# A hybrid decoder layer on one core: the gate map stored by groups of four blocks, the residual loaded earlier, the softmax exponential moved up, and the sample tokens' expert rows spread over more groups

## The chip, the cores and the metric

The kernel runs on one core of a Trainium2 chip. The metric is the device time of one execution in microseconds. Three runs of the kernel before gave 5026.5, 5029.96 and 5038.7 us, so the median is 5029.96 us. One further execution was taken with the profiler; its times are those of the trace.

## What is computed

One decoder layer is applied to 512 prompt tokens and 64 sample tokens (576 together, model width 2048): a pooling and retention mixer, a cross-attention over memory tokens, and the PEER expert mixer, with a normalization ahead of each and one at the end. The change lies in the last of them:

```python
def one(xb):
    q = (xb @ peer_wq).reshape(PEER_BLOCK, PEER_HEADS, 2, PEER_HALF)
    s = jnp.einsum('thcd,hckd->thck', q, subkeys)      # 8 heads, 2 x 128 keys
    sv, si = lax.top_k(s, PEER_TOPK)                   # 16 of each
    cand = sv[:, :, 0, :, None] + sv[:, :, 1, None, :]
    ...
    top_s, sel = lax.top_k(cand, PEER_TOPK)            # 16 experts per head
    expert = jnp.take_along_axis(cidx, sel, axis=-1)   # of 16384
    g = jax.nn.softmax(top_s, axis=-1)
    u = jnp.take(peer_u, expert, axis=0)
    act = jax.nn.gelu(jnp.einsum('thkd,td->thk', u, xb), approximate=False)
    vv = jnp.take(peer_v, expert, axis=0)
    return jnp.einsum('thk,thkd->td', g * act, vv)
```

So every token has 128 chosen experts, each with a gate; the result is added to the residual, and the final normalization follows.

## The kernel before

The 16384 experts are 128 blocks of 128. The tokens are handled in two ways. For 320 of them ("dense", `ND`) all experts are computed: the activations of a block by matmul with `uT`, an elementwise product with a map of the gates (zero where an expert was not chosen), and a matmul with `vE`, whose 16 output pieces DVE adds to the residual `X`. For the other 256 (`NG`, two chunks of 128) the activations of all experts are computed, but of `vE` only the chosen rows are used: POOL gathers, for each of the 128 places in a token's list, one row of 2048 values per token (1 MB per gather, `row`, L463), and DVE adds it, times its weight, to `ACC` in PSUM (`add_row`, L1637). The weights come from 256 small gathers (`value`, L453). Weights of all matmuls are split into a high and a low part so that the product keeps float32 accuracy: ACT copies the high part (L882), POOL subtracts to get the low part (`low_part`, L417), and each 128x128 block is multiplied three times (L535, L850).

The stages of this part, one after the other:

1. **Heads**: a loop over eight heads. PE projects the queries, then computes the activations for the 256 tokens, in eight pairs of blocks per head (`tokens_first`, L779; on ACT `gelu_tokens`). DVE finds the top 16. After the loop ACT takes the exponential of the softmax (L1211), DVE normalizes it, PE turns the lists (L811), ACT copies them out, and DVE signals `lists_ready`.
2. **Map**: ten steps (`NPG`) of 32 dense tokens. DVE builds one-hot matrices, PE multiplies them to the gate map (L825), ACT copies it to `STG` (two halves `par`) and stores each half to `pmap` in DRAM (L1231, 2 MB each); in between PE computes the activations of two expert blocks per step, so that ten pairs are done ahead (`LAG`). POOL issues ten values per step.
3. **Groups**: 27 (`QT`) groups of four blocks (`quad`). PE does four projections (two calls of `up`, 192 matmuls), then `down` (192 matmuls, 16 pieces d = 0 to 15). POOL has 16 low parts per group, in the order k = 0 to 15: k = 0 to 7 for the next projections, 8 to 15 for the next `down`; after which k it issues rows and values is written out by hand. Two consecutive k feed one half of a matmul stage, and the four slots of `WS` are used in turn, so that POOL can work on a slot only when PE has left it and ACT has written its high part. ACT and POOL have one queue each, in order; a wait holds all that is behind it.
4. **Tail**: five (`NQ - QT`) groups with `down` alone, since their projections were done ahead; then the final normalization.

The rows: each of the two chunks has 128; each group takes `KR` = 10, so that chunk 0 is spread over groups 0 to 12, chunk 1 over groups 13 to 25, and group 26 and the tail have none. When a chunk is complete, ACT copies `ACC` (`rows_evac`), PE turns it in 16 transposes after d = 13 of that group's `down` (L859), and DVE adds it to `X` (L1699). Five buffers hold rows that are on their way (`NB`).

At the turn from map to groups ACT waits for the last stores to `pmap`, issues the loads for group 0 (`load_quad`, L1241 and L1243), then the four loads of the residual (`load_x` of `x3T`, L293), and then goes on to the first projection's output (`gelu_out`, L1192, whose result `store_gelu` writes to `gel`).

## Time and profile before

| | |
|---|---|
| median of three runs | 5029.96 us (5026.5 to 5038.7) |
| the profiled execution, its own time | 5085.41 us |
| its span | 5083.6 us |
| mean granted TensorE clock | 0.948 of full |
| PE busy / weight load busy | 93% / 89% of the span |
| POOL / DVE / ACT busy | 61% / 45% / 31% |
| moved by DMA | 1033 MB, 203 GB/s on average |
| heads end, map begins | about 2947 to 2957 us |
| map ends, groups begin | about 3250 us |
| first `down` | 3308.06 us |
| groups end, tail begins | about 4907 us |

The profiled execution is 55 us (1.1%) longer than the median. A time in this text is a moment or a duration in its trace; 0 is the start of the span. A busy share is an average over the stages and says little about what ends a stage: that is read from the idle time in front of an instruction and from what ended it.

### The profile page before, as it was taken

The numbers are of one execution on the slowest core, as the hardware profiler recorded it, in microseconds if no ns is written. First come the engines' busy times: TensorE is split into PE (matmuls) and PEld (weight loads), VectorE is DVE, ScalarE is ACT, GpSimd is POOL, SyncE is SP. The second block draws the span as 40 slices with busy tenths as digits, with TensorE's granted clock in tenths as the row PEclk, the third lists the DMA queues.
The fourth block names the chain that finished last, engine by engine and source line by source line (L and its number), as shares of the span: only waits on it lengthen the run. The fifth ranks groups of instructions, "written<-read, shape, count | busy, mean of one in ns | idle before, by whom it ended". The sixth has DMA issues, their size and how long they took to land.

```text
span 5083.6 us, 83212 instructions
## 1 busy us (share of the span) xinstructions
PE 4704.6 (93%) x32243; PEld 4538.4 (89%) x32243; DVE 2306.8 (45%) x3103; ACT 1579.4 (31%) x2182; POOL 3100.8 (61%) x1782
## 2 busy tenths in 40 slices
PE   7978999899899998999999988799999999999997
PEld 7778889889788797999999988699999999999997
DVE  3622222422200115444444445366666666666656
ACT  4411112212211223444444444333333333333333
POOL 6723222224211144777777766589999889998864
PEclk9989889899988899999999988899999999999998
DMA  6533222433343424555555545699999899999954
GB/s 217 181 68 95 85 69 85 131 106 105 122 140 139 153 84 149 176 172 171 174 172 173 174 141 165 217 340 345 347 344 343 323 342 342 341 341 356 362 192 148
DMA packets 466619, 1033.07 MB, mean 203 GB/s; under 512 B 136945, under 2 KB 227185, under 8 KB 433649
## 3 DMA queue, kind: packets, MB, share of 16 engines
q1 hardware_dynamic: 216080, 590.67, 34.9%
q0 software_dynamic: 45056, 268.60, 13.8%
q10 hardware_dynamic: 205280, 170.84, 10.4%
q8 instruction: 159, 2.61, 0.2%
q14 instruction: 44, 0.35, 0.0%
HBM read 935.25 MB, written 94.73 MB: 203 GB/s over the span
## 4 chain that ended last, share of the span: by engine, by line
issue 41%; POOL 33%; PE 17%; DMA 3%; DVE 2%; another core or an unknown queue 1%; ACT 1%; ACTq 0%; POOLq 0%; DVEq 0%; SPq 0%
POOL WS L417 22%; PE PS L850 9%; POOL WS L441 7%; PE PS L535 5%; POOL ROWS L463 2%; DMA AR<-in_vE 2%; PE PS L779 2%; POOL AR L453 2%; PE PS L825 1%; ACT WS L882 1%; DMA RAW<-in_vE 1%; DMA gel<-AR 0%; POOL AR L463 0%; DVE AR L1331 0%
## 5 line engine op out<-in xcount | busy, mean ns | idle before, releaser
L535 PE MATMUL PS<-HL,WS 128*128 128x288 f32 (+2 forms) x16896 | 2409.1, 304 | 121.5 <-issue 41.5
L535 PEld LDWEIGHTS PS<-HL,WS 128*128 128x128 f32 x16896 | 2361.7, 191 | 145.6 <-issue 107.1
L417 POOL TENSOR_TENSOR WS<-RAW,WS 128x1024 fp32r<-128x1024 f32 x490 | 1203.0, 2468 | 1572.9 <-ACT WS L882 1569.9
L850 PE MATMUL PS<-WW,WS 128*128 128x320 f32 x6144 | 944.4, 316 | 77.6 <-POOL WS L417 61.6
L850 PEld LDWEIGHTS PS<-WW,WS 128*128 128x128 f32 x6144 | 925.2, 192 | 96.2 <-issue 81.2
L882 ACT ACTIVATE WS<-RAW 128x1024 fp32r<-128x1024 f32 (+1 forms) x714 | 627.1, 919 | 915.3 <-PE PS L535 279.3
L779 PE MATMUL PS<-WS,HL 128*128 128x256 f32 x6144 | 740.5, 283 | 0.0
L779 PEld LDWEIGHTS PS<-WS,HL 128*128 128x128 f32 x6144 | 738.3, 192 | 0.0
L1637 DVE SCALAR_TENSOR_TENSOR PS<-ROWS,AR,PS 128x2048 f32<-128x2048 f32 x206 | 483.8, 2348 | 73.0 <-DMA ROWS<-in_vE,AR 72.2
L417 POOL TENSOR_TENSOR WS<-AR,WS 128x1024 fp32r<-128x1024 f32 x182 | 450.1, 2478 | 34.2 <-ACT WS L882 33.3
L417 POOL TENSOR_TENSOR WS<-CS,WS 128x1024 fp32r<-128x1024 f32 x144 | 347.5, 2413 | 195.1 <-ACT WS L882 193.4
L1652 DVE TENSOR_TENSOR AR<-AR,PS 128x320 f32<-128x320 f32 x512 | 248.6, 486 | 436.0 <-PE PS L850 433.4
L882 ACT ACTIVATE AR<-PS 128x512 f32<-128x512 f32 (+12 forms) x243 | 169.6, 737 | 842.5 <-PE PS L535 410.5
L882 ACT ACTIVATE WS<-CS 128x1024 fp32r<-128x1024 f32 (+1 forms) x256 | 222.9, 871 | 498.2 <-PE PS L850 255.6
L441 POOL TENSOR_TENSOR WS<-RAW,WS 128x512 fp32r<-128x512 f32 x224 | 302.5, 1379 | 16.1 <-ACT WS L882 15.3
L453 POOL DMA_INDIRECT AR<-gelg,AR x256 | 249.4, 974 | 70.6 <-issue 65.4
L882 ACT ACTIVATE WS<-AR 128x1024 fp32r<-128x1024 f32 (+1 forms) x294 | 259.7, 888 | 93.1 <-DMA AR<-in_vE 35.8
L1541 DVE MAX8 AR<-AR 128x8 f32<-128x128 f32 (+1 forms) x120 | 30.1, 324 | 488.7 <-ACT AR L882 487.5
L463 POOL DMA_INDIRECT ROWS<-in_vE,AR x206 | 200.2, 972 | 31.9 <-issue 24.4
L1192 ACT ACTIVATE AR<-PS 128x320 f32<-128x320 f32 x128 | 56.7, 443 | 459.7 <-PE PS L535 396.2
L1625 DVE TENSOR_TENSOR AR<-AR 128x320 f32<-128x320 f32 x128 | 193.9, 1566 | 0.1
L1637 DVE SCALAR_TENSOR_TENSOR PS<-AR,PS 128x2048 f32<-128x2048 f32 x50 | 117.6, 2353 | 120.7 <-DMA AR<-in_vE,AR 120.7
(160 smaller groups left out, 3196.9 us busy)
## 6 DMA issues: line engine op xcount, KB each, us to landing
RAW<-in_uT SPq DMA_DIRECT2D x256, 512.0 KB
RAW<-in_w_lin SPq DMA_DIRECT2D x218, 512.0 KB
CS<-in_uT SPq DMA_DIRECT2D x128, 512.0 KB
AR<-in_uT SPq DMA_DIRECT2D x128, 512.0 KB
RAW<-in_vE SPq DMA_DIRECT2D x128, 512.0 KB
CS<-in_vE SPq DMA_DIRECT2D x64, 512.0 KB
AR<-in_vE SPq DMA_DIRECT2D x64, 512.0 KB
AR<-in_w_lin SPq DMA_DIRECT2D x46, 512.0 KB
```

Of the source, the lines that this page charges most:

```text
L417: pool.tensor_tensor(WS[:, k, 1, :], raw(k, many, late), WS[:, k, 0, :].bitcast(F32), ALU.subtract)\
L441: pool.tensor_tensor(WS[:, k, 1, half], raw(k, True, True)[:, half], WS[:, k, 0, half].bitcast(F32), ALU.subtract).then_inc(S["split_done" ...
L453: pool.indirect_dma_start(out=GA[:, c, k:k + 1], out_offset=None, in_=values, in_offset=at(EL[:, c, k:k + 1]))\
L463: pool.indirect_dma_start(out=ROWS[b], out_offset=None, in_=rows, in_offset=at(VI[:, c, r:r + 1]))\
L535: ins = mm(to, WS[:, slot + hf, wp, k * P:(k + 1) * P], x, start=first and (wp, xp) == (0, 0), stop=last and wp == 1, skip_group_check=True)
L779: ins = mm(to, HLG[:, c, xp, kb, :], WS[:, 2 * hf:2 * hf + 2, wp, k * P:(k + 1) * P], start=(kb, c, wp, xp) == (0, 0, 0, 0), stop=kb == KB ...
L850: ins = mm(bank(2 + d % 2, ND), WS[:, 2 * (q % 2) + b, vp, 512 * e + P * d4:512 * e + P * (d4 + 1)], W[:, 2 * b + e, wp, :], start=(b, e, ...
L882: copy = lambda out, in_, **kw: act.activation(out, in_, ACT.Identity, **kw)
L1192: act.activation(GO[:, e, :], bank(e, ND), ACT.Gelu).then_inc(S["lin_evac"], 1)
L1625: tt(gi, gi, PP[:, e // 2, :, e % 2, :], ALU.mult).then_inc(S["w_done"], 1)
L1637: stt(ACC, ROWS[b], GA[:, c, r:r + 1], ACC, ALU.mult, ALU.add).then_inc(S["row_done"], 1)
L1652: tt(X[:, d, 0:ND], X[:, d, 0:ND], bank(2 + d % 2, ND), ALU.add).then_inc(S["v_free"], 1)
```

## The change

Four things are changed:

- The map is stored for groups of four blocks: `pmap` is (32, 128, 10, 128) in place of (64, 128, 10, 64), so each piece that a store writes is 128 values instead of 64 (10 stores of 2 MB as before). `STG` now lies in `ROWS4`, where the gathered rows will be; the one-hot matrices and lists move as well.
- That frees the place of `X`: the residual is loaded at the start of the map stage, after `lists_ready`, and not at its end. At the turn to the groups, ACT takes the first two outputs of group 0 before it waits for the stores and issues the loads for group 0. The first row of `vE` can be gathered only when the last store is done, so POOL waits for it after k = 9 of group 0.
- The exponential is issued on ACT ahead of the last pair of blocks of the last head; that head is written outside the loop for it.
- Rows: two in group 0, nine in each of the groups 1 to 26 (chunk 0 up to group 14, chunk 1 from group 15), and 20 in the first four tail groups, five each. DVE adds the tail's after d = 4, 5, 10, 12 and 14. Chunk 1 is turned in the last `down` after d = 5 and added after d = 7, and the squares of the final normalization wait for that (`back_added`).

```diff
-KR = 2 * NB
-QR = -(-P // KR)
+KR = 9
+QA = 15
+FIRST_ROWS = P - KR * (QA - 1)
...
-        pmap = dram("pmap", (NP2, P, NPG, 2 * PG))
+        pmap = dram("pmap", (NQ, P, NPG, 4 * PG))
...
-        AA, BB, STG = ar(1152, 2, 4, P), ar(2176, 2, 4, P), ar(3200, 2, NK, PG)
+        AA, BB = ar(10432, 2, 4, P), ar(11456, 2, 4, P)
+        STG = ROWS4.rearrange("p (s i t) -> p s i t", s=2, i=NK)
...
+            def rows_after(i, k, many):
+
+                for j, (c, r) in enumerate(ROWS_OF[i]):
+                    if k == (10 + 2 * j if i == 0 else many * j // KR if i < QT else many * j // KT_ROWS):
+                        row(c, r)
+
             for i in range(QT):
-                c, first = i // QR, i % QR * KR
                 for k in range(16):
                     low_part(H_UV + 16 * i + k // 4 * 4, k % 4, late=True)
-                    for j in range(KR):
-                        if c < 2 and first + j < P and 8 * j // 5 == k:
-                            row(c, first + j)
+                    if i == 0 and k == 9:
+                        for par in range(2):
+                            pool.wait_ge(S[f"out_p{par}"], 16 + 16 * (NPG // 2))
+                    rows_after(i, k, 16)
...
-                        if back and d == 13:
+                        if back and d == (13, 5)[back - 1]:
                             pe.wait_ge(S["rows_evac"], back)
...
                 for j in range(UPP):
+                    if last and j == UPP - 1:
+                        act.wait_ge(S["soft_in"], 1)
+                        act.activation(CAND.rearrange("p t n -> p (t n)")[:, 0:640], EQ.rearrange("p a n -> p (a n)")[:, 0:640],
+                                       ACT.Exp).then_inc(S["soft_exp"], 1)
                     gelu_tokens(h, j)
...
             copy(IOTA4, IOTA.unsqueeze(1).to_broadcast([P, 4, P])).then_inc(S["gt_evac"], 1)
+            act.wait_ge(S["lists_ready"], 1)
+            load_x(act, x3T)
...
                         if (a, e) == (1, 0) and not first:
                             load_next(i + 1)
+                        if (a, e) == (0, 1) and first:
+                            for par in range(2):
+                                act.wait_ge(S[f"out_p{par}"], 16 + 16 * (NPG // 2))
+                            load_quad(0)
...
-            for par in range(2):
-                act.wait_ge(S[f"out_p{par}"], 16 + 16 * (NPG // 2))
-            load_quad(0)
-            load_x(act, x3T)
...
+                    if q == 0 and i == NQ - 1:
+                        evac_rows(1)
+
+
+            act.wait_ge(S["back_added"], 1)
...
                     if d % 3 == 2:
-                        add_rows(i, (NB + d // 3,))
+                        add_rows(i, (5 + d // 3 if i else d // 3 - 3,))
...
+                    if d in (4, 5, 10, 12, 14):
+                        add_rows(i, ((4, 5, 10, 12, 14).index(d),))
+                    if i == NQ - 1 and d == 7:
+                        add_back(1).then_inc(S["back_added"], 1)
```

**ACT, turn from map to groups.** Before (`gel` stores, `pmap` and `gel` loads, `x3T` loads, then the outputs of group 0; "waits" are semaphores):

```order
L1241 DMA AR<-pmap 128x2x640 [waits out_p1,out_g0,out_p0,out_g1,out_gg1,out_gg0]
L1243 DMA AR<-gel 128x4x320
L293 DMA AR<-x3T 128x4x576 x4
L1192 ACTIVATE AR<-PS 128x320 [waits out_g0,used]
L882 ACTIVATE WS<-RAW 128x1024 [waits raw0]
L882 ACTIVATE WS<-RAW 128x1024 [waits raw1]
L1197 DMA gel<-AR 128x320 [waits lin_evac]
L1192 ACTIVATE AR<-PS 128x320 [waits out_g1,used]
L882 ACTIVATE WS<-CS 128x1024 [waits raw2]
```

And now:

```order
L1206 ACTIVATE AR<-PS 128x320 [waits out_g0,used]
L896 ACTIVATE WS<-RAW 128x1024 [waits raw0]
L896 ACTIVATE WS<-RAW 128x1024 [waits raw1]
L1211 DMA gel<-AR 128x320 [waits lin_evac]
L1206 ACTIVATE AR<-PS 128x320 [waits out_g1,used]
L896 ACTIVATE WS<-CS 128x1024 [waits raw2]
L896 ACTIVATE WS<-AR 128x1024 [waits raw3]
L1211 DMA gel<-AR 128x320 [waits lin_evac]
L1260 DMA AR<-pmap 128x1280 [waits out_g0,out_g1,out_p1,out_p0]
L1262 DMA AR<-gel 128x4x320
```

The wait for the stores stands behind the first two outputs, and the four loads of `x3T` are gone from here.

**POOL, a group in the middle, k = 4 to 8** (a TENSOR_TENSOR is a low part, a DMA from `in_vE` a row, one from `gelg` a value). Before:

```order
L417 TENSOR_TENSOR WS<-RAW,WS 128x1024 [waits hi_done]
L463 DMA ROWS<-in_vE,AR 128x2048 [waits row_done]
L417 TENSOR_TENSOR WS<-RAW,WS 128x1024 [waits hi_done]
L453 DMA AR<-gelg,AR 128x1
L417 TENSOR_TENSOR WS<-CS,WS 128x1024 [waits hi_done]
L463 DMA AR<-in_vE,AR 128x2048 [waits row_done]
L417 TENSOR_TENSOR WS<-AR,WS 128x1024 [waits hi_done]
L453 DMA AR<-gelg,AR 128x1
L417 TENSOR_TENSOR WS<-RAW,WS 128x1024 [waits hi_done]
L463 DMA ROWS<-in_vE,AR 128x2048 [waits row_done]
```

And now:

```order
L425 TENSOR_TENSOR WS<-RAW,WS 128x1024 [waits hi_done] x2
L471 DMA AR<-in_vE,AR 128x2048 [waits row_done]
L461 DMA AR<-gelg,AR 128x1
L425 TENSOR_TENSOR WS<-CS,WS 128x1024 [waits hi_done]
L425 TENSOR_TENSOR WS<-AR,WS 128x1024 [waits hi_done]
L471 DMA ROWS<-in_vE,AR 128x2048 [waits row_done]
L461 DMA AR<-gelg,AR 128x1
L425 TENSOR_TENSOR WS<-RAW,WS 128x1024 [waits hi_done]
L471 DMA ROWS<-in_vE,AR 128x2048 [waits row_done]
```

The fourth and the fifth row of the group stand one low part later; their number here is the same.

**POOL, the same group, from k = 9 to the row behind k = 12.** Before:

```order
L417 TENSOR_TENSOR WS<-RAW,WS 128x1024 [waits hi_done]
L463 DMA ROWS<-in_vE,AR 128x2048 [waits row_done]
L453 DMA AR<-gelg,AR 128x1
L417 TENSOR_TENSOR WS<-CS,WS 128x1024 [waits hi_done]
L417 TENSOR_TENSOR WS<-AR,WS 128x1024 [waits hi_done]
L463 DMA ROWS<-in_vE,AR 128x2048 [waits row_done]
L453 DMA AR<-gelg,AR 128x1
L417 TENSOR_TENSOR WS<-RAW,WS 128x1024 [waits hi_done]
L463 DMA ROWS<-in_vE,AR 128x2048 [waits row_done]
```

And now:

```order
L425 TENSOR_TENSOR WS<-RAW,WS 128x1024 [waits hi_done]
L461 DMA AR<-gelg,AR 128x1
L425 TENSOR_TENSOR WS<-CS,WS 128x1024 [waits hi_done]
L471 DMA ROWS<-in_vE,AR 128x2048 [waits row_done]
L425 TENSOR_TENSOR WS<-AR,WS 128x1024 [waits hi_done]
L461 DMA AR<-gelg,AR 128x1
L425 TENSOR_TENSOR WS<-RAW,WS 128x1024 [waits hi_done]
L471 DMA ROWS<-in_vE,AR 128x2048 [waits row_done]
```

Here, between k = 9 and k = 12, stands the row that each group has lost.

## Rows read from the trace of the kernel before

**Rows 1.** The page: busy time, share, instructions.

```profile
PE 4704.6 (93%) x32243; PEld 4538.4 (89%) x32243; DVE 2306.8 (45%) x3103; ACT 1579.4 (31%) x2182; POOL 3100.8 (61%) x1782
```

**Rows 2.** Timeline, PE, heads to map: start, us, instructions, [idle before <-releaser].

```profile
2879.82 67.36 PE L779 MATMUL PS<-WS,HL 128*128 128x256 f32 x560
2954.73 2.18 PE L811 MATMUL PS<-CST,AR 128*128 128x128 f32 x9 [7.55 <-DVE AR L1596]
```

**Rows 3.** Timeline, ACT and then DVE, same place.

```profile
2941.54 2.01 ACT L882 ACTIVATE WS<-RAW 128x1024 fp32r<-128x1024 f32 x2 [4.20 <-PE PS L779]
...
2950.49 1.28 ACT L1211 ACT_TABLE_LOAD   x1 [0.71 <-ACT AR L1183]
2951.79 0.74 ACT L1211 ACTIVATE AR<-AR 128x640 f32<-128x640 f32 x1
...
2952.55 0.82 DVE L1594 TENSOR_REDUCE AR<-AR 128x40 f32<-128x640 f32 x1 [32.58 <-ACT AR L1211]
```

**Rows 4.** Timeline, PE, map to groups.

```profile
3250.17 14.32 PE L535 MATMUL PS<-HL,WS 128*128 128x320 f32 x96
3280.41 15.81 PE L535 MATMUL PS<-HL,WS 128*128 128x320 f32 x96 [15.92 <-POOL WS L417]
3308.06 15.63 PE L850 MATMUL PS<-WW,WS 128*128 128x320 f32 x96 [11.84 <-DVE WW L1630]
```

**Rows 5.** Timeline, ACT, same place.

```profile
3252.47 0.39 ACTq L1231 DMA_DIRECT2D pmap<-AR  x1
...
3269.86 0.41 ACTq L1241 DMA_DIRECT2D AR<-pmap  x1
...
3270.82 5.61 ACTq L293 DMA_DIRECT2D AR<-x3T  x4
...
3298.89 0.44 ACT L1192 ACTIVATE AR<-PS 128x320 f32<-128x320 f32 x1 [17.25 <-DMA gel<-AR]
...
3303.33 1.54 ACT L882 ACTIVATE WW<-AR 128x320 fp32r<-128x320 f32 x4
```

**Rows 6.** Timeline, PE, a usual group, and the `down` of another.

```profile
3703.20 28.32 PE L535 MATMUL PS<-HL,WS 128*128 128x320 f32 x192
3733.74 15.88 PE L850 MATMUL PS<-WW,WS 128*128 128x320 f32 x96 [2.22 <-POOL WS L417]
...
3612.45 14.48 PE L850 MATMUL PS<-WW,WS 128*128 128x320 f32 x96 [2.20 <-POOL WS L417]
```

**Rows 7.** Timeline, POOL: k = 9, k = 12 of one group, the row behind.

```profile
3731.25 2.36 POOL L417 TENSOR_TENSOR WS<-RAW,WS 128x1024 fp32r<-128x1024 f32 x1
...
3743.84 2.40 POOL L417 TENSOR_TENSOR WS<-RAW,WS 128x1024 fp32r<-128x1024 f32 x1 [0.70 <-ACT WS L882]
3746.39 0.95 POOL L463 DMA_INDIRECT ROWS<-in_vE,AR  x1
```

**Rows 8.** Timeline, DVE, same group: fifth row added, first piece of `down`.

```profile
3730.75 2.35 DVE L1637 SCALAR_TENSOR_TENSOR PS<-AR,PS 128x2048 f32<-128x2048 f32 x1 [3.66 <-DMA AR<-in_vE,AR]
3736.96 0.49 DVE L1652 TENSOR_TENSOR AR<-AR,PS 128x320 f32<-128x320 f32 x1 [3.85 <-PE PS L850]
```

**Rows 9.** Waits, 3425 to 4925 us: total, times, longest.

```profile
DVE PS L1637 <- DMA AR<-in_vE,AR: 111.7, 24, 5.7
```

**Rows 10.** Stretches: length, busy (count) of each engine, clock, DMA share, GB/s.

```profile
3700.00:3760.90 60.90, 58.40 (x385) 57.80 (x385) 40.88 (x35) 19.25 (x24) 55.20 (x33) 0.97 0.93 344
...
4661.00:4722.00 61.00, 59.49 (x403) 58.80 (x402) 41.26 (x37) 20.13 (x25) 51.32 (x28) 1.00 0.97 367
...
4905.00:4935.00 30.00, 29.89 (x203) 29.42 (x202) 17.16 (x25) 9.48 (x12) 20.87 (x9) 1.00 0.61 201
```

**Rows 11.** Timeline, POOL in the tail; then PE in the last `down`, and transposes.

```profile
4901.88 4.78 POOL L417 TENSOR_TENSOR WS<-RAW,WS 128x1024 fp32r<-128x1024 f32 x2 [2.52 <-ACT WS L882]
...
5043.76 10.60 PE L850 MATMUL PS<-WW,WS 128*128 128x320 f32 x60 [1.94 <-DVE AR L1652]
...
4844.83 1.97 PE L859 MATMUL PS<-CST,AR 128*128 128x128 f32 x16 [0.35 <-ACT AR L882]
```

More of the change, by code:

```diff
@@ L867, in quad @@
                 down(n + 8, i, WW, back)
-            for c in range(2):
-                with pe.Fori(0, QR - 1) as i:
-                    quad(i + c * QR)
-                quad(c * QR + QR - 1, back=c + 1)
-            for i in range(2 * QR, QT):
+            with pe.Fori(0, QA - 1) as i:
                 quad(i)
+            quad(QA - 1, back=1)
+            with pe.Fori(0, QT - QA) as i:
+                quad(i + QA)
             for i in range(QT, NQ):
-                down(H_V + 8 * (i - QT), i, (WW, WW2)[(i - QT + 1) % 2])
+                down(H_V + 8 * (i - QT), i, (WW, WW2)[(i - QT + 1) % 2], back=2 * (i == NQ - 1))
             norm_sum(4)
@@ L1198, in store_gelu, with head @@
                     .then_inc(S[f"out_g{e}"], 16)
-            with act.Fori(0, EH) as h:
+            def head(h, last=False):
                 act.wait_ge(S["sk_done"], h + 1)
@@ L1639, in add_rows, with add_back @@
             def add_rows(i, js):
-                c, first = i // QR, i % QR * KR
                 for j in js:
-                    if c < 2 and first + j < P:
-                        add_row(c, first + j)
+                    if 0 <= j < len(ROWS_OF[i]):
+                        add_row(*ROWS_OF[i][j])
+            def add_back(c):
+                dve.wait_ge(S["back_done"], c + 1)
+                x = X[:, :, ND + P * c:ND + P * (c + 1)]
+                return tt(x, x, ACC.rearrange("p (c n) -> p c n", c=KB), ALU.add)
             def sums(i, n, after):
@@ L1694, in _ @@
                 sums(i, H_UV + 16 * i + 8, after)
[L1695 to L1702 removed]
+                if i == QA - 1:
+                    step.hold(step.mark(add_back(0)))
+                    link(dve.memset(ACC, 0.0))
             for i in range(QT, NQ):
```

68 lines of the change are left out of this document (32 added, 36 removed).

## The prediction, made before the changed kernel was run

> **What bounds the kernel now.** I read the page first: PE is busy 93% of the span, so what a change can win is idle PE time or a lowered clock, and POOL, at 61%, is the only other engine that can be a bound over a long stretch [rows 1]. Then the timeline of PE, for the stretches without matmuls, and beside each the engine that ended it. There are three such places that the change touches.
>
> First, heads to map: PE stops at 2879.82 + 67.36 = 2947.18 and starts at 2954.73, ended by DVE [rows 2]. DVE had been waiting 32.58 us for ACT's exponential, so it had been ready since 2920; ACT took the exponential only at 2951.79, behind its last work for the heads [rows 3].
>
> Second, map to groups: PE finishes group 0's first two projections at 3264.5, waits 15.92 us for POOL, does the other two, waits 11.84 us for DVE, and starts the first `down` at 3308.06 [rows 4]. Behind both waits stands ACT: the last store of the map is issued at 3252.47, ACT is released at 3269.86, spends 5.61 us on issuing the loads of the residual, and later waits 17.25 us for a small `gel` store, which is queued behind those loads [rows 5].
>
> Third, the groups: each lasts 60.9 us, for PE does 28.3 us of projections, waits 2.2 us for POOL, and then runs the first half of `down` in 15.9 us; in 7 of the 22 groups that still issue values that half takes 14.5 us after the same wait [rows 6]. The granted clock is 0.97 in such a group, and 1.00 in a late one, where the values are done [rows 10]. So POOL sets the pace of some 22 groups, and nearly nothing but PE that of the rest and of the tail.
>
> **The change part by part.**
>
> *Exponential.* It moves to where ACT has 4.20 us of idle time; it costs a table load and itself, 1.28 + 0.74 = 2.0 us [rows 3], and is hidden there; without that idle time it would hold ACT's next high parts, and so PE, by these 2 us. DVE then has its sums and the normalized gates before PE ends the heads. What goes is the 7.55 us; what is late next is ACT's last output of the heads (now with a table load back, 1.28), then its copy of the lists. ACT's issue of the residual's loads comes right behind, 5.6 us by [rows 5], while the first map copies become due about 4 us later: up to 1.6 us of it shows. 7.5 - 1.3 - 1.2 = **5 us** gained, between 2 and 7.
>
> *Turn to the groups.* ACT now takes the outputs of the first two projections at about 3257.5 and 3264.5, as PE finishes them. POOL needs two low parts of 2.4 us per projection, PE 7.2 us per projection, as within any group, so PE runs all four without a stop, 3250.2 + 28.3, plus 1 for small waits: 3279.5. ACT has meanwhile waited until 3269.9 for the last store, if that stays as slow as now, and issued the loads for group 0; they carry 1.3 MB, and nothing large is ahead of them. From ACT's last output to the first `down` the work is that of now: it takes that output at about 3301.1, PE starts at 3308.06, so 7 us, in which lie 1.54 us for the high parts [rows 5] and DVE's low parts. 3279.5 + 7 + 0.5 = 3287, against 3308: **21 us** gained. Bounds: 24 if the stretch has no small waits and one copy less, 16 if the products, which DVE can begin only when the loads have landed, are 5 us late. The residual's 4.7 MB are hidden in the map stage, whose DMA is half idle; if that cover were gone, they would cost the 14 us that 4.7 MB take at 344 GB/s [rows 10]. POOL's new wait after k = 9 of group 0 has values, six low parts and the rows of that group behind it; it is passed at about 3280, ten microseconds after the stores, so it costs nothing.
>
> The store itself: it takes 3269.86 - 3252.47 = 17.4 us for 2.1 MB in pieces of 256 bytes [rows 5]. The Trainium skill (DMA: Bandwidth & Descriptors, Specifications) says that pieces under 512 bytes are handled by read-modify-write, and so below line rate; the new ones have 512. By that rule ACT is released some microseconds sooner and the products cannot be late; by the row the release stays at 3270. Between the two lies at most 1 us of the sum, since ACT gets to that wait only at 3267.
>
> *Nine rows per group.* This looks like 1.1 us of POOL time (0.95 and the 0.16 ahead of it) per group, but it depends on where it is. The loop that closes is: POOL's k = 0 to 9, which PE waits for; then the first quarter of `down`; ACT's high part; k = 12, row, k = 13; another quarter; ACT; k = 0 of the next group. In k = 0 to 9 there are six rows ahead of the end of k = 9, before as after. The row that goes stands between k = 9 and k = 12. From the end of k = 9 at 3733.61 to k = 12 at 3743.84 there are 10.23 us, of which POOL is idle for the last 0.70 [rows 7]: it waits for PE there, and a row less makes it wait longer. Only in the 7 groups with the fast first half is it different: there PE's way is 15.88 - 14.48 = 1.4 us shorter, 8.8 us, POOL's own is 9.5 and becomes 8.4, so 0.7 us can be won, 5 us in all. I take **3 us**, since the loads of `vE` must then come sooner too. Bounds: 0, and 25 us if each of the 22 groups gives back its 1.1.
>
> That the clock falls after the wait is what the trace shows in 15 groups of 22 [rows 6]. The Trainium skill (TensorE: Matmul & The Clock Gate, HAM oscillation) says that a PE that idles between tiles pays for it again with a stretch at half clock (1.2 instead of 2.4 GHz). If each wait of 2.2 us did so, there would be no fast groups, this term would be 0 and the time 3 us higher; the trace agrees only for the 15.
>
> The fifth row is issued about 2.5 us later than now. DVE waits 3.66 us for it, adds it until 3733.10, and then waits 3.85 us for the first piece [rows 8]; the mean wait is 111.7/24 = 4.7, the longest 5.7 [rows 9]. 2.5 us later, even in the longest case, DVE is 0.7 us late for piece 0, whose bank PE needs only for piece 2, 1.8 us after that. So nothing, with a slope behind it. Group 14, where chunk 0 is turned, now has its last row after d = 11 instead of d = 8; its add (2.35) and ACT's copy then end after d = 13: **1.5 us** lost, 0 to 3.
>
> *Twenty rows in the tail.* They have less cover than a group gives. Per `down`: POOL has about 2.5 us idle per quarter [rows 11] and gets 1.1 per row, but the row behind the first low part of a pair makes the second late: PE's quarter lasts 7.2 us, ACT and the pair with a row 1.1 + 4.8 + 1.1 = 7.0, so 0 to 1 us, I take 0.7. DVE is busy 17.2 of 30 us [rows 10] and gets 5 x 2.35 = 11.8: 29 of 30, full but for 1 us, and the pieces have a second bank as cover. DMA carries 201 GB/s and gets 5.2 MB per 29 us, 181 GB/s: 382, where the fastest stretch shows 367 at a share of 0.97 [rows 10]; that is 378 at a full share, so 1% too much, 0.3 to 2 us in each of the first three. Together 4 x 0.7 + 3 x 0.7 = **5 us** lost; 1 to 12.
>
> *End.* The 16 transposes, 1.97 + 0.35 us [rows 11], move from group 25 to the last `down`. There PE is already held by DVE (1.94 us), which adds squares from d = 8 on; the addition of chunk 1, 2.3 us as any pass over 2048 values [rows 8], now stands ahead of it, and ACT's squares wait for it. **2 us** lost, 0 to 5. Group 26 gets nine rows and loses nothing that its neighbours don't.
>
> Sum: -5 - 21 - 3 + 1.5 + 5 + 2 = -20.5 us. It is made against the profiled execution (5085.4 us, to 5065). That is 55 us above the median; I have no sign that these places differ without the profiler, so I carry the difference over: 5030 - 20.5 = **5009 us**.
>
> **The rivals.** (a) Every group gains its 1.1 us: the sum becomes -5 - 21 - 25 + 8.5 = -42.5, so 4987 us. For it: POOL fills 55.2 of 60.9 us [rows 10]. Against: the 0.70 us of idle at k = 12. (b) The turn gains only 10 us, since after the removal of ACT's wait the loads for group 0, the products and the first loads of `vE` come together: 5020. For it: DMA is the fullest there. Against: what filled it, the residual and five rows, is gone. (c) The tail is bound by DVE and DMA: each of four `down`s is 5 us longer instead of 1.2: 5024. For it: the two sums of 29 of 30 us and 382 GB/s. (d) The other side: the fifth row lands too late. DVE is in order, so piece 0 waits behind it, and PE stops at piece 2. It decides once the row lands more than 3 us later, in relation to its issue, than in [rows 9]; at 5.5 us later PE loses 2.5 us in each of 26 groups, 65 us: 5077. Against: 5% less is gathered per group. (e) That the change doesn't do what it says is hardly possible for the rows and the loads, which the order of the instructions shows; for the larger pieces it would change nothing here, as the store isn't waited for longer than PE works.
>
> **How the numbers follow.** Forecast 0.60 (its own range 5001 to 5018), (a) 0.10, (b) 0.12, (c) 0.13, (d) 0.05. The range reaches from (a) to (c) and a little beyond: 4988 to 5026. A difference of 0.3% is 15 us, about what a measurement of this kernel can tell from none: faster means below 5015. That takes five sixths of the forecast, (a), and a third of (b) and (c): 0.50 + 0.10 + 0.08 = 0.68. The same: 0.26. Slower, (d): 0.06.
>
> **What would show it.** PE's stop between heads and map is 2 to 4 us. The first `down` starts 35 to 37 us after the map's last store is issued, not 55.6. The groups with values still last 60 to 61 us, with the 2.2 us wait for POOL, and POOL is idle longer ahead of k = 12. `down`s of the tail last 29.5 to 30.5 us. It would be wrong if the waits of `down` for POOL became shorter than 1.5 us (a), if DVE showed waits for a row with PE waiting for DVE behind them (d), or if PE stood still in group 0 for more than 10 us (b).

## The result, and the profile after

| | before | after |
|---|---|---|
| median in the same set of runs | 5037.52 us (six runs) | 5061.19 us (5047.52 to 5071.94, six runs) |
| ratio | | 1.0051, 95% interval 1.0031 to 1.0070 |
| profiled execution | 5085.41 us | 5067.45 us |

The changed kernel is slower by 0.5% (24 us by the medians, 26 by the ratio), where 20 us less was forecast. The two profiled executions say the opposite, 18 us less. That is the first thing to clear up: the profile of before has 70 us more in the map stage than any other profile of a kernel with that map stage, bar one set of runs (see e2, e3 and the last section). So the traces have to be compared by stretch, and the map stage left out.

Four stretches, each read off PE's timeline: **turn**, from the first projection of group 0 to the first `down`; **groups**, from the first `down` to the projections of group 26; **tail**, from there to the end of the last `down`; **end**, the rest of the span.

| us | before | after | difference | forecast |
|---|---|---|---|---|
| end of heads to first map product | 14.3 | 8.9 | -5.4 | -5 |
| turn | 57.9 | 36.9 | -21.0 | -21 |
| groups | 1542.1 | 1573.3 | +31.2 | -3 + 1.5 |
| tail | 204.2 | 232.0 | +27.8 | +5 |
| end | 29.2 | 31.0 | +1.8 | +2 |

The sum of the differences is +34.4 us; the timed runs have 24 to 26. These are single traces, and the groups and the tail of the changed kernel come out 7 and 3 us shorter in a second one (end of the next section). Three rows came out as forecast, and the other two are off by 33 and 23 us.

In the page of after, the busy times say nothing of this: PE 4704.6 became 4689.0, and POOL is as before [rows 1].

```profile
PE 4689.0 (93%) x32243; PEld 4515.4 (89%) x32243; DVE 2365.1 (47%) x3102; ACT 1564.3 (31%) x2171; POOL 3100.0 (61%) x1782
```

**What went as forecast.** Timeline of PE, from the heads to the first `down` (start, us, instructions, idle before and what ended it):

```profile
2964.28 1.15 PE L826 MATMUL PS<-CST,AR 128*128 128x128 f32 x9
...
2973.35 2.08 PE L840 MATMUL PS<-AR 128*128 128x128 f32 x8 [6.17 <-DVE AR L1643]
...
3192.47 28.42 PE L550 MATMUL PS<-HL,WS 128*128 128x320 f32 x192 [0.33 <-POOL WS L425]
3229.36 17.07 PE L865 MATMUL PS<-WW,WS 128*128 128x320 f32 x96 [8.47 <-DVE WW L1654]
```

PE now turns the lists with no stop (7.55 us in [rows 2]) and pays 6.17 us later (1.59 before), for ACT has a last output of the heads and its copies still to do. That makes 3.0 us less idle time. Another 2.2 of the 5.4 us are in the matmuls between: the nine that turn the lists and the twelve behind them took 5.12 us before, at a mean granted clock of 0.54 behind PE's stop, and take 2.90 now, at 1.00, with no stop ahead of them. The four projections run as one piece; 15.92 us of waiting for POOL are gone [rows 4]. And ACT at the same place:

```profile
2956.33 0.74 ACT L1225 ACTIVATE AR<-AR 128x640 f32<-128x640 f32 x1
...
3194.23 0.39 ACTq L1252 DMA_DIRECT2D pmap<-ROWS  x1
...
3210.00 0.35 ACTq L1260 DMA_DIRECT2D AR<-pmap  x1
```

From the last store of the map to the first `down` it is 3229.36 - 3194.23 = 35.1 us (35 to 37 forecast; 55.6 before).

**What did not.** A usual group, PE:

```profile
3659.76 14.42 PE L865 MATMUL PS<-WW,WS 128*128 128x320 f32 x96 [2.12 <-POOL WS L425]
3675.13 5.55 PE L865 MATMUL PS<-WW,WS 128*128 128x320 f32 x36 [0.95 <-DVE AR L1680]
3681.48 9.18 PE L865 MATMUL PS<-WW,WS 128*128 128x320 f32 x60 [0.81 <-DVE AR L1680]
```

In this group the wait for POOL ahead of `down` is as in [rows 6]; in 9 of the 21 groups behind group 0 it is under 1.5 us. New are two waits for DVE in the second half. What DVE was doing, and when POOL had issued the rows (POOL's issues behind k = 10 and k = 12, then DVE's additions of these two rows):

```profile
3663.36 0.95 POOL L471 DMA_INDIRECT ROWS<-in_vE,AR  x1 [0.16 <-issue]
...
3670.88 0.95 POOL L471 DMA_INDIRECT ROWS<-in_vE,AR  x1
...
3672.33 2.35 DVE L1661 SCALAR_TENSOR_TENSOR PS<-ROWS,AR,PS 128x2048 f32<-128x2048 f32 x1 [1.14 <-DMA ROWS<-in_vE,AR]
...
3678.68 2.35 DVE L1661 SCALAR_TENSOR_TENSOR PS<-ROWS,AR,PS 128x2048 f32<-128x2048 f32 x1 [1.00 <-DMA ROWS<-in_vE,AR]
```

These two rows are there 9.0 and 7.8 us after their issue; the median is 8.2 (e4). Nine rows over sixteen low parts are issued after k = 0, 1, 3, 5, 7, 8, 10, 12, 14; the ten of before after 0, 1, 3, 4, 6, 8, 9, 11, 12, 14. So from the fourth row on, each one but the sixth comes one or two low parts later, while DVE adds it at the same place of `down`. DVE then stands in front of a sum, and PE behind it for its bank.

The tail, two moments: PE's first `down` there, and one of the four with rows.

```profile
4844.98 16.57 PE L865 MATMUL PS<-WW,WS 128*128 128x320 f32 x96 [7.98 <-DVE AR L1680]
4864.15 10.35 PE L865 MATMUL PS<-WW,WS 128*128 128x320 f32 x60 [2.59 <-DVE AR L1680]
...
4889.83 5.70 PE L865 MATMUL PS<-WW,WS 128*128 128x320 f32 x36 [0.71 <-DVE AR L1680]
4897.11 9.05 PE L865 MATMUL PS<-WW,WS 128*128 128x320 f32 x60 [1.58 <-DVE AR L1680]
4906.52 14.31 PE L865 MATMUL PS<-WW,WS 128*128 128x320 f32 x96 [0.35 <-POOL WS L425]
```

A `down` of the tail takes 31.7 us (4906.52 - 4874.82, the starts of two second halves). Before, 1044 matmuls took 155.94 us, 28.7 for 192:

```profile
4885.88 155.94 PE L850 MATMUL PS<-WW,WS 128*128 128x320 f32 x1044 [0.37 <-DVE AR L1652]
```

PE's new waits in such a `down` are 0.71 and 1.58 us for DVE, 2.3 of the 3.0 us.

### The profile page after: what moved, and what is told of

The parts are those of the page before. It is cut to its first block, busy times and chain, and to the rows that moved or that the text cites. A ratio compares the mean times of both kernels' runs of the same rounds, so it can differ in the third digit from the quotient of the medians.

```text
span 5065.6 us, 83187 instructions
## 1 busy us (share of the span) xinstructions
PE 4689.0 (93%) x32243; PEld 4515.4 (89%) x32243; DVE 2365.1 (47%) x3102; ACT 1564.3 (31%) x2171; POOL 3100.0 (61%) x1782
## 4 chain that ended last, share of the span: by engine, by line
issue 40%; POOL 37%; PE 12%; DMA 5%; DVE 4%; ACT 1%; POOLq 0%; SPq 0%; ACTq 0%; DVEq 0%
POOL WS L425 24%; POOL WS L449 7%; PE PS L865 7%; PE PS L550 3%; POOL AR L461 3%; DMA ROWS<-in_vE,AR 3%; POOL ROWS L471 2%; PE PS L794 2%; DVE PS L1661 2%; ACT WS L896 1%; DMA RAW<-in_vE 1%; DMA AR<-in_vE,AR 1%; DVE WW L1654 1%; POOL AR L471 0%; DVE AR L1355 0%
## 5 line engine op out<-in xcount | busy, mean ns | idle before, releaser
L865 PEld LDWEIGHTS PS<-WW,WS 128*128 128x128 f32 x6144 | 911.8, 190 | 161.3 <-DVE AR L1680 95.2
L449 POOL TENSOR_TENSOR WS<-RAW,WS 128x512 fp32r<-128x512 f32 x224 | 302.9, 1381 | 15.6 <-ACT WS L896 14.7
L896 ACT ACTIVATE AR<-PS 128x256 f32<-128x256 f32 (+11 forms) x163 | 83.7, 555 | 699.7 <-PE PS L550 413.3
L1654 DVE TENSOR_TENSOR WW<-AR,WW 128x320 fp32r<-128x320 f32 x128 | 250.5, 1990 | 3.0 <-ACT WW L896 2.6
L449 POOL TENSOR_TENSOR WS<-CS,WS 128x512 fp32r<-128x512 f32 x112 | 159.7, 1426 | 11.5 <-ACT WS L896 11.0
```

The source lines that it names most:

```text
L449: pool.tensor_tensor(WS[:, k, 1, half], raw(k, True, True)[:, half], WS[:, k, 0, half].bitcast(F32), ALU.subtract).then_inc(S["split_done" ...
L865: ins = mm(bank(2 + d % 2, ND), WS[:, 2 * (q % 2) + b, vp, 512 * e + P * d4:512 * e + P * (d4 + 1)], W[:, 2 * b + e, wp, :], start=(b, e, ...
L896: copy = lambda out, in_, **kw: act.activation(out, in_, ACT.Identity, **kw)
L1654: tt(W[:, e, 1, :], GI[:, e, :], W[:, e, 0, :].bitcast(F32), ALU.subtract).then_inc(S["ww_ready"], 1)
```

## The experiments

Two theories stood at the start, called L and M in the expectations below. **Rows** (L): the whole loss is in where rows are issued and added, and the rest of the change gains what the traces show. **Rest** (M): the turn, the map stage or the new format give nothing or lose when no profiler runs. Each ratio is that to the kernel before on the same chip; the table is at the end of this section.

**e1: the rows as before.** The changed kernel with ten rows per group, at the old places, and none in the tail.

```diff
-KR = 9
-QA = 15
+KR = 10
+QA = 14
...
-                    if k == (10 + 2 * j if i == 0 else many * j // KR if i < QT else many * j // KT_ROWS):
+                    if k == (10 + 2 * j if i == 0 else 8 * j // 5):
```

> The changed kernel with its rows as in the kernel before: two in group 0, ten in each later group, issued after the same low parts as there (k = 0, 1, 3, 4, 6, 8, 9, 11, 12, 14), none in the tail; chunk 0 is complete in group 13 and chunk 1 in group 26. Map format, early residual and exponential stay. Theory L (the loss is in the rows: late rows hold DVE in the groups, and the tail has no room for 20): all of the loss goes and the gain of the turn is left, 5010 to 5018 us where the kernel before has 5037, ratio 0.994 to 0.996; groups of 60.9 us and tail downs of 28.8 us in the trace. Rival M (the turn and the map stage gain nothing outside the profiler, or lose): 5035 to 5061, ratio 1.000 or above.

Measured: 5013.60 us against 5029.81, ratio 0.9965 (0.9951 to 0.9978). Its ratio is below those of both kernels. The gain is a little less than expected, which fits the trace: group 26 now has rows and the turn of chunk 1, and the tail is 215.9 us, not 204.2.

**e2: the rows alone.** The kernel before with `KR`, `ROWS_OF`, the tail's rows and the late turn of chunk 1, and nothing else of the change.

```diff
-KR = 2 * NB
-QR = -(-P // KR)
+KR = 9
+QA = 15
...
-                        if back and d == 13:
+                        if back and d == (13, 5)[back - 1]:
```

> The kernel before with the rows of the changed kernel alone: two in group 0, nine in each later group at the changed places, twenty in the tail, chunk 1 turned in the last down. Map, residual and exponential as before. Theory L: all of the loss is here, the 31 us of the groups and 28 us of the tail that the two traces show, so 5085 to 5097 us, ratio 1.009 to 1.012. Rival M: the loss comes mainly from the other parts, so at most 5050.

Measured: 5071.83 us, ratio 1.0089 (1.0074 to 1.0104), 45 us lost by the ratio, just short of the 1.009 to 1.012 expected. With e1's gain of 18 us that makes +27, and the change as a whole measures +26: the two parts add up, and Rest has fallen. (Its turn is 50.9 us, not 57.9: with two rows in group 0 instead of ten, part of the turn's gain comes from the rows.)

**e3: the format alone.**

```diff
-        pmap = dram("pmap", (NP2, P, NPG, 2 * PG))
+        pmap = dram("pmap", (NQ, P, NPG, 4 * PG))
...
-                    tt(gi, gi, PP[:, e // 2, :, e % 2, :], ALU.mult).then_inc(S["w_done"], 1)
+                    tt(gi, gi, PP[:, :, e, :], ALU.mult).then_inc(S["w_done"], 1)
```

> The kernel before with the map's format alone: stored by groups of four blocks, in pieces of 512 bytes instead of 256, loaded accordingly. Theory P (the stalls of 6 to 9 us per half step of the map, seen in the profiled execution of the kernel before only, come from the 256-byte pieces while profiling): the time stays, ratio 0.998 to 1.001, and in the profile a half step takes 21.8 us as in the changed kernel instead of 29.4, so that the profiled execution is 5030 to 5040 us. Rival Q (the stalls come from something else that the change moves): the profiled execution stays at 5085. Rival R (the stalls exist outside the profiler too): the time falls by 30 us or more.

Measured: 5031.74 us, ratio 1.0006 (0.9997 to 1.0015), and no stalls, span 5033.1. So far theory P. But e2 still has the small pieces, and its profile has no stalls either: its map stage, first to last product, takes 214.9 us, and e3's takes 214.9. P has fallen. What the pieces do cost is DMA time; e2 first, then e3 (length, busy of PE, PEld, DVE, ACT, POOL, clock, DMA share, GB/s):

```profile
2900.00:3180.00 280.00, 267.68 (x2026) 265.69 (x2025) 178.29 (x269) 168.84 (x191) 232.50 (x171) 0.99 0.67 189
```

```profile
2900.00:3180.00 280.00, 267.87 (x2037) 265.88 (x2037) 182.39 (x299) 166.20 (x192) 234.16 (x170) 0.98 0.60 189
```

The same 189 GB/s need a share of 0.67 in the one and 0.60 in the other (from the first to the last map product, 0.69 and 0.61). That agrees with the rule on pieces under 512 bytes that the prediction cites from the Trainium skill (DMA: Bandwidth & Descriptors, Specifications). The kernel's time doesn't change by it. Nor is the last store released sooner: from its issue to the first load of group 0 it takes 22.1 us in e3, with 512 bytes, where it takes 17.4 before and 15.6 in e2, with 256, and e3's turn is 61.3 us, longer than the 57.9 of before. What holds that store in e3 is open.

**e4: the nine rows at earlier places.** The changed kernel, rows after k = 0, 1, 3, 4, 6, 8, 9, 11, 12.

```diff
-                    if k == (10 + 2 * j if i == 0 else many * j // KR if i < QT else many * j // KT_ROWS):
+                    if k == (10 + 2 * j if i == 0 else 8 * j // 5 if i < QT else many * j // KT_ROWS):
```

> The changed kernel, only its nine rows per group are issued after the low parts k = 0, 1, 3, 4, 6, 8, 9, 11, 12 as in the kernel before, and not after 0, 1, 3, 5, 7, 8, 10, 12, 14. The tail stays. Theory L: the rows land early enough for the additions again, the 31 us of the groups go mostly: 5035 to 5045 us, 15 to 25 below the changed kernel, ratio 1.000 to 1.002. Rival K (the groups are longer for another reason, such as vector additions that have become longer): 5055 to 5065, ratio about 1.005.

Measured: 5025.01 us, ratio 0.9990 (0.9980 to 1.0000), better than the 1.000 to 1.002 expected, and the groups take 1541.9 us. One expression is worth 31 us of the groups (24 against the second trace of the changed kernel). K has fallen.

**e5: the exponential alone.** The kernel before with the last head outside the loop and the exponential ahead of its last pair.

```diff
+                    if last and j == UPP - 1:
+                        act.wait_ge(S["soft_in"], 1)
+                        act.activation(CAND.rearrange("p t n -> p (t n)")[:, 0:640], EQ.rearrange("p a n -> p (a n)")[:, 0:640],
+                                       ACT.Exp).then_inc(S["soft_exp"], 1)
                     gelu_tokens(h, j)
```

> The kernel before with the exponential alone moved ahead of the last pair of the last head. Theory: PE's way from the end of the heads to the first map product becomes 5 us shorter (14.3 us in the runs with the old place, 9.1 in the changed kernel), so 5022 to 5027 us, ratio 0.998 to 1.000. It also tests the odd map stage of the first profile: theory S (those nine stalls belonged to that one execution): this profile has none of them and its execution is within 15 us of its median. Rival: the stalls come back and the profiled execution is about 5080.

Measured: ratio 0.9996 (0.9984 to 1.0009); 5 us are within that. The trace shows them: 9.07 us from the turning of the lists to the first map product and no stop ahead of the turning, where it was 7.55 + 6.71. The stalls came back, so S as it was put, one odd execution, has fallen too (last section). In this set of runs (e5 to e8) every kernel took some 60 us more than elsewhere, the kernel before 5093 us, so only its ratios are used.

**e6 and e9: which rows.** Rows after k = 0, 1, 3, 5, 7, 8, 9, 11, 12 (e6: fourth and fifth late, the end restored), and after 0, 1, 3, 4, 6, 8, 10, 12, 14 (e9: the reverse).

```diff
-                    if k == (10 + 2 * j if i == 0 else many * j // KR if i < QT else many * j // KT_ROWS):
+                    if k == (10 + 2 * j if i == 0 else (0, 1, 3, 5, 7, 8, 9, 11, 12)[j] if i < QT else many * j // KT_ROWS):
```

> The changed kernel with the rows of the second half of a group restored: rows j = 0 to 8 are issued after k = 0, 1, 3, 5, 7, 8, 9, 11, 12 (the kernel before: 0, 1, 3, 4, 6, 8, 9, 11, 12; the changed one: 0, 1, 3, 5, 7, 8, 10, 12, 14). Theory L2 (the loss in the groups comes from rows j = 6 to 8, which DVE waits for between the sums of the second half of down): nearly all of the 31 us returns, 5025 to 5033 us, ratio 0.999 to 1.001. Rival D (it comes from the fourth and fifth rows, which are now issued after k = 5 and 7 and hold up piece 0): stays near the changed kernel, 5048 to 5060, ratio 1.004 or more.

> The changed kernel with the rows of the first part of a group restored and those of the second left late: j = 0 to 8 after k = 0, 1, 3, 4, 6, 8, 10, 12, 14. It is the counterpart of e6 (5, 7 late and the end restored), whose groups still took 22 us more than those of the kernel before, from first down to last projections 1562 against 1542 us; the changed kernel has 1573. Theory A (both halves cost their own part): 1550 to 1555 us for that stretch, PE waiting for DVE's sums in the second half, ratio to the kernel before 1.000 to 1.002. Rival B (the late fourth and fifth rows alone push everything): 1542 to 1545, ratio 0.999 or less. Rival C (the second half alone is as bad): 1565 or more.

Measured: e6 1.0046 (1.0028 to 1.0064) and 1562.3 us for the groups, +20 over e4; e9 1.0016 (1.0005 to 1.0026) and 1553.4 us, +11.5. L2 has fallen as the whole story; both halves cost their own part (theory A of e9), and the fourth and fifth rows the larger, by the traces and by the ratios. But not in the way that I had thought. Waits over groups 1 to 20 (total us, times, longest) of e4:

```profile
PE PS L865 <- POOL WS L425: 61.5, 40, 2.2
...
ACT WS L896 <- DMA CS<-in_vE: 15.4, 10, 3.0
```

of e6:

```profile
PE PS L865 <- POOL WS L425: 74.3, 41, 2.9
...
ACT WS L896 <- DMA CS<-in_vE: 64.9, 18, 4.7
...
PE PS L865 <- DVE AR L1680: 0.2, 1, 0.2
```

of e9, and of the changed kernel:

```profile
PE PS L865 <- DVE AR L1680: 33.0, 43, 2.2
PE PS L865 <- POOL WS L425: 27.3, 22, 1.9
```

```profile
PE PS L865 <- DVE AR L1680: 41.9, 48, 3.0
PE PS L865 <- POOL WS L425: 38.0, 24, 2.1
```

With the fourth and fifth rows late (e6), PE does not wait for DVE at all: ACT waits for the weights of the second half (64.9 us instead of 15.4), POOL for ACT, and PE for POOL. With the last rows late (e9), PE waits 33 us for DVE, but 34 us less for POOL, since a `down` that is held in its second half gives POOL time; the loss is then at the ends: group 14, where chunk 0 is turned (67.3 us; 63.1 in e4), group 1 (63.5; 60.5) and the last four groups (59.4 to 60.3; 57.8 to 58.6). The changed kernel has both, and PE waits 80 us, 18 more than in e4. DVE's waits for rows are not longer in sum: 203 us in the changed kernel, 218 in e4 over the same 20 groups. What has changed is where in `down` they fall. That moved rows stand in front of the weights in the DMA engines would explain e6; the runs show the wait, not the order of the packets.

**e7: the tail's additions without its gathers** (on e4).

```diff
                     low_part(H_V + 8 * (i - QT) + k // 4 * 4, k % 4, late=True)
-                    rows_after(i, k, 8)
...
-                dve.wait_ge(S[f"in_row{b}"], 16 * (before + r // NB + 1))
+                if not c or r < P - 20:
+                    dve.wait_ge(S[f"in_row{b}"], 16 * (before + r // NB + 1))
```

> The kernel with earlier rows (e4) where the tail's 20 rows are not gathered: POOL issues nothing for them, and DVE makes its 20 additions at the same places from what the row buffers hold, so chunk 1's last 20 rows are wrong data; nothing else is left out. Theory V (the tail's downs are set by DVE: additions two in a row plus products and low parts that are stretched beside POOL's low parts): downs stay at 31 us or more, time 5018 to 5026. Rival G (gathers or POOL's issues set them): downs 28.5 to 29.5 us, time 5010 to 5016.

Measured: ratio 0.9998 (0.9986 to 1.0010); tail 223.3 us where e4 has 226.7, a `down` 30.4 us (4950.99 - 4920.56) instead of 31.7. Neither as it was put: of the 3 us that such a `down` is too long, the additions make 1.7, the gathers and their issue 1.3, by the traces; the ratios of e4 and e7 can't tell so small a difference. Part of the 1.3 can be seen on DVE, which is slowed beside POOL. DVE and POOL in one `down` of e4, DVE first:

```profile
4889.04 0.49 DVE L1654 TENSOR_TENSOR WW<-AR,WW 128x320 fp32r<-128x320 f32 x1
4889.44 0.49 DVE L1680 TENSOR_TENSOR AR<-AR,PS 128x320 f32<-128x320 f32 x1
4889.84 2.66 DVE L1654 TENSOR_TENSOR WW<-AR,WW 128x320 fp32r<-128x320 f32 x1
...
4892.82 3.27 DVE L1654 TENSOR_TENSOR WW<-AR,WW 128x320 fp32r<-128x320 f32 x1
```

```profile
4889.74 2.42 POOL L425 TENSOR_TENSOR WS<-CS,WS 128x1024 fp32r<-128x1024 f32 x1 [1.08 <-ACT WS L896]
4892.29 1.03 POOL L471 DMA_INDIRECT ROWS<-in_vE,AR  x1
4893.35 2.38 POOL L425 TENSOR_TENSOR WS<-AR,WS 128x1024 fp32r<-128x1024 f32 x1
```

The same operation, 128x320 from two operands in SBUF, takes 0.49 us while POOL is idle and 2.66 or 3.27 us beside one of POOL's low parts: it ends 0.3 to 0.4 us after POOL's does (4892.50 after 4892.16; 4896.09 after 4895.73). A sum with an operand in PSUM stays at 0.49. The Trainium skill (SBUF — State Buffer, SBUF: two separate sides) has it as an exclusive lock, held for a whole instruction, between GpSimd reading SBUF and a VectorE operation with two SBUF inputs; the one that starts first gets it. The trace agrees: in the changed kernel 14 such operations that DVE entered with POOL idle, less than 0.5 us ahead of a low part of POOL, took 0.48 to 0.49 us. The second operation above was entered 0.5 us before POOL's low part and still waited, but POOL was not idle then: it was issuing a row. Whether that issue takes part in the lock no run shows; most operations that DVE enters beside an issue take 0.48 us. In e7, where POOL issues no row there, the second low part takes 2.29 us, and PE's wait behind it is 0.58 instead of 1.57 us: that is 1.0 of the 1.3.

How much DVE is slowed in sum decides nothing. Over 21 groups a low part takes 1.09 us and a product, slowed in the same way, 1.72 before; in the changed kernel it is 2.17 and 1.11; in e4, whose groups last as long as before, 1.37 and 0.49. In these traces work that POOL slows costs time where a sum that PE waits for stands behind it.

**e8: another order on DVE in the tail** (on e4).

```diff
-                if i < NQ and 6 <= d < 10:
-                    lows_w(i, (d - 6,), W)
+                if i < NQ and d in (10, 11, 12):
+                    lows_w(i, ((0,), (1, 2), (3,))[d - 10], W)
...
-                    if d in (4, 5, 10, 12, 14):
-                        add_rows(i, ((4, 5, 10, 12, 14).index(d),))
+                    if d in (4, 6, 8, 13, 14):
+                        add_rows(i, ((4, 6, 8, 13, 14).index(d),))
```

> The kernel with earlier rows (e4) with another order on DVE in the tail: the four low parts of the next weights after d = 10, 11, 11, 12, where POOL has some 4 us without a low part, not after d = 6 to 9, and the five rows after d = 4, 6, 8, 13, 14 instead of 4, 5, 10, 12, 14. Theory O (what counts is the order: a row beside a stretched low part makes a sum late): tail downs 29 to 30 us instead of 31.7, time 5013 to 5020, ratio 0.997 to 0.998. Rival T (the total of DVE's work, 28 of 31.7 us, sets the down whatever the order): 31 us or more per down, time 5023 to 5028.

Measured: slower, ratio 1.0024 (1.0015 to 1.0034), tail 240.8 us. DVE's part went as hoped: one low part takes 1.35 us, the others 0.48, and PE hardly waits for it. But, on ACT and then on PE:

```profile
4925.03 0.34 ACTq L1260 DMA_DIRECT2D AR<-pmap  x1
4925.40 1.02 ACTq L1262 DMA_DIRECT2D AR<-gel  x1
4926.52 2.01 ACT L896 ACTIVATE WS<-RAW 128x1024 fp32r<-128x1024 f32 x2 [9.63 <-issue]
...
4933.78 17.03 PE L865 MATMUL PS<-WW,WS 128*128 128x320 f32 x96 [4.43 <-POOL WS L425]
```

I had overlooked who waits for the low parts: ACT issues the next loads only when they are done (`load_next` waits for `ww_ready`; DVE's last one ends at 4924.99, the load is issued at 4925.03), and its high parts, POOL and PE stand behind that. So neither O nor T is decided by the time; the run shows a dependence that bars this order.

**e10: the hand-over to the tail** (on e1), for group 26 alone.

```diff
-                        if (a, e) == (1, 0) and not first:
+                        if (a, e) == ((0, 1) if isinstance(i, int) and i == QT - 1 else (1, 0)) and not first:
                             load_next(i + 1)
...
                 lows_w(i, (2, 3), WW)
+                if i == QT - 1:
+                    add_rows(i, (0, 1))
```

> The kernel with ten rows per group (e1), and in group 26 alone two things moved: ACT issues the loads for the first tail group after its second output, not its third, and DVE makes the low parts of that group's weights ahead of its first rows. In e1 DVE waited 8.3 us for these loads behind the first sum of group 26 (issue to landing 17 us), and PE 6.3 + 1.4 us for DVE. Theory: the loads land some 7 us sooner, those waits go and the clock stays up, so 7 to 10 us less than e1: ratio 0.994 to 0.996. Rival: the loads queue behind the rows anyway and land when they did, ratio 0.9965 as e1.

Measured: 5004.05 us against 5027.74, ratio 0.9952 (0.9937 to 0.9968), the lowest of all; the interval overlaps that of e1, so that it is better than e1 rests on the tail in the trace, 208.7 us instead of 215.9. The run makes both moves at once and doesn't tell them apart. In e1 the load is issued at the first line and DVE has it at the second; e10 (behind it) issues it 15.9 us into group 26 instead of 22.7, and DVE waits no more:

```profile
4795.15 0.50 ACTq L1261 DMA_DIRECT2D AR<-gel  x1
...
4812.28 0.49 DVE L1648 TENSOR_TENSOR AR<-AR 128x320 f32<-128x320 f32 x1 [8.34 <-DMA AR<-gel]
```

```profile
4782.27 0.66 ACTq L1261 DMA_DIRECT2D AR<-gel  x1
...
4797.82 1.22 DVE L1648 TENSOR_TENSOR AR<-AR 128x320 f32<-128x320 f32 x1
```

**The changed kernel once more.**

> The changed kernel as it is, once more, beside the kernel before on the same chip. Ratio 1.004 to 1.007 as at first, whether or not this chip is one on which the map stage shows stalls (280 to 288 us from first to last map product in e5 to e8 and in the first profile of the kernel before, 215 to 218 in the others): groups 1573 us and tail 232 us as in its first profile.

Measured: 1.0058 (1.0038 to 1.0078); groups 1566.2 us, tail 228.6. So a stretch repeats within some 7 us in this kernel. Group 14, 67.7 us in the first trace, is 64.2 here.

| us | turn | groups | tail | ratio |
|---|---|---|---|---|
| before | 57.9 | 1542.1 | 204.2 | 1 |
| after | 36.9 | 1573.3 | 232.0 | 1.0051 |
| after again | 36.9 | 1566.2 | 228.6 | 1.0058 |
| e1 ten rows | 36.9 | 1546.9 | 215.9 | 0.9965 |
| e2 rows alone | 50.9 | 1565.0 | 233.8 | 1.0089 |
| e3 format alone | 61.3 | 1543.0 | 204.2 | 1.0006 |
| e4 rows earlier | 36.9 | 1541.9 | 226.7 | 0.9990 |
| e5 exponential | 57.4 | 1540.2 | 204.3 | 0.9996 |
| e6 fourth, fifth late | 36.9 | 1562.3 | 232.1 | 1.0046 |
| e7 no gathers in tail | 36.9 | 1542.6 | 223.3 | 0.9998 |
| e8 tail's order | 36.9 | 1542.3 | 240.8 | 1.0024 |
| e9 last rows late | 36.9 | 1553.4 | 225.9 | 1.0016 |
| e10 early load | 36.9 | 1543.2 | 208.7 | 0.9952 |

## Why the prediction was wrong

The forecast was 5009 us (4988 to 5026), faster at 0.68. It came out at 5061, outside the range, and slower, which had 0.06.

- **Exponential**: the number was right, -5 forecast, -5.4 in the traces of after and e5 (too small to show in e5's time), but in part by luck. PE's stop ahead of the first product is 6.2 us, not the 2 to 4 that I had set as the sign, so only 3.0 us of idle time went. Another 2.2 us came from the granted clock, 1.00 instead of 0.54 while PE turned the lists, for which the sum has no term.
- **Turn**: right. -21 forecast, -21.0 measured, and the times on PE and ACT are those that the prediction gives. Rival (b), that only 10 would be gained, is out. Two things make the exact match worth less: two rows in group 0 instead of ten gain 7 us by themselves (e2), for which the sum has no term, and in e3, the kernel before but for the format, the turn takes 61.3 us.
- **Nine rows per group**: the step that failed. The count was sized rightly, within what a trace can tell: with the rows at the places of before (e4) the groups change by -0.2 us, turn of chunk 0 included, where -3 and +1.5 stood. But the change also moves the rows, and I priced one of the moved ones, the fifth, against piece 0. The order of the instructions shows four others moved: the fourth, and those now behind k = 10, 12 and 14. Their additions stand at fixed pieces of `down`, some 8 us behind the issue, and in [rows 8] and [rows 9] I looked only at the row ahead of piece 0. A look at the issue and the addition of each row, k by k, would have shown that. Cost: 31 us in the first trace, 24 in the second.
- **Fifth row, rival (d)**: the direction was right and had 0.05. Late fourth and fifth rows cost 20 us over the groups (e6), not 65, and by way of late weights, not of DVE at piece 0. Its condition, a row that lands more than 3 us later in relation to its issue, was not needed.
- **The turn of chunk 0** in group 14: +1.5 forecast; that group takes 67.7 us (64.2 in the second trace) against 62.8 for the group of before that does the same (group 12). It is 63.1 in e4: the rest is again rows that are issued late.
- **Tail**: a term that was mis-sized, +5 forecast, +27.8 measured. It has three parts. Group 26, of which I wrote that it "loses nothing that its neighbours don't", costs 11.7 us without a single row in the tail (e1 against e3; e1 also turns chunk 1 there), and 7.2 of them go when the loads for the tail are issued earlier and their low parts made ahead of the first rows (e10). The tail's rows themselves cost 10.8 (e4 against e1); such a `down` is 3.0 us longer than before, not 1.2. I had DVE at 29 of 30 us, and took the average for the limit; what decides is that two additions in a row (PE waits 0.7 us behind them) and the stretched low parts (1.6 us) stand ahead of a sum. And 5.3 come from the late places in group 26 (after against e4), by the fourth and fifth rows: e6 has them, e9 has not. Rival (c) had the right place and 5 us per `down`, but not group 26.
- **End**: the number was right, +2 and +1.8, by luck. e1, which has no turn in the last `down`, has 31.0 too, and e10, whose last `down` and end are those of e1, has 29.2. The four matmuls of the last normalization take 2.29 us in e1 and in after, at a granted clock of 0.5, and 1.24 in e10 and before, at 1.0; PE's wait ahead of them is 3.37 instead of 2.62 us. So most of the 1.8 us goes with the clock at that moment, which the sum did not contain, and the chunk that is turned doesn't show.
- **Carrying the profile's surplus over**: it did no harm to the differences, for the stretches concerned were not in the map stage. But the 55 us were not spread over the kernel, as I let it stand: they lay in one stage (last section).

By the conditions I had set: PE's stop between heads and map was to be 2 to 4 us, the groups with values were to last 60 to 61 us, and the tail's `down`s 29.5 to 30.5; all three are missed. "DVE showed waits for a row with PE waiting for DVE behind them" is what the trace of after shows. The sign of rival (a), waits of `down` for POOL under 1.5 us, shows too, in 9 of 21 groups, but not for its reason: in e4, with the same nine rows, 20 of the 21 waits are 2.0 to 2.2 us. A `down` that is held in its second half gives POOL that time.

## What to carry to other kernels

Where gathers are issued by one engine and used by another at fixed places, write down for each one the time from issue to use before and after, and compare it with the landing time in the trace; a formula that spreads fewer gathers evenly moves nearly all of them, and here that alone cost 31 us. Work taken from one place must be priced at the place where it lands, with the loads that now queue behind it: e1 and e10 keep ten rows per group, leave the tail free, and are 0.35 and 0.48% faster than the kernel before. And when a profiled execution is 1% off the median, find the stage that holds the difference before a sum is made on it.

## What the runs showed of the hardware

- **Stalls of PE, ACT and DVE in the map stage.** In the first profile of before (whose timed runs, at 5030 us, can hardly have had it) and in all four of e5 to e8, the map stage takes 280 to 288 us from first to last product; in the other eight it takes 215 to 218. The waits of e6 in that stage, with no local releaser:

```profile
DVE PS L1640 <- remote: 86.9, 10, 8.9
ACT ROWS L896 <- remote: 75.3, 10, 8.5
```

  In these moments PE issues single matmuls with gaps of up to 1.6 us and no semaphore to wait for, and POOL's values go on. It was there for all kernels of one set of runs (the kernel before too, at 5093 us), with pieces of 256 and of 512 bytes, and for none of the next set, on the same chip. The cause is open; no run tells it.
- A gather of 1 MB lands 8.2 us (median, e4 in the groups) after its issue while DMA is busy at 0.89, and the load of 640 KB from `gel` 17.3 us after (median, the changed kernel, DMA at 0.88).
- An operation on DVE, 128x320 with two operands in SBUF, takes 0.49 us by itself, up to 3.27 beside one of POOL's low parts, and 5.68 beside two of them in a row (a product in the kernel before, with a row's issue under way when DVE entered it); with one operand in PSUM it never took more than 0.49 (494 of them, e4 from the groups on).
- The granted clock had fallen behind a stop: the 21 matmuls at the turn from heads to map took 5.12 us at 0.54 behind a stop of 7.55 us, and 2.90 at 1.00 without that stop.
